# A decoder layer on one core: three more k pairs of the MLP's down product in seven products, and halves added by DMAs

## What is computed

```python
x = _layer_norm(DEEPNORM_ALPHA * x + xa, ln2_g[l], ln2_b[l])
ff = jnp.square(jax.nn.relu(x @ w_ff1[l])) @ w_ff2[l]      # 1024 -> 4096 -> 1024
x = _layer_norm(DEEPNORM_ALPHA * x + ff, ln3_g[l], ln3_b[l])
```

## Time and profile before

| | us |
|---|---|
| median of 3 runs (lowest, highest) | 400.83 (400.57, 403.71) |
| the profiled execution | 401.14 |
| its span, first to last instruction | 399.3 |
| PE, DVE, ACT busy in the span | 390.9, 330.2, 251.3 |

### The profile page before, as it was taken

How to read it: one execution, slowest core, us unless ns; L and a number is a source line. 1 busy time by engine, 2 the same in 40 slices (tenths; PEclk the granted TensorE clock), 3 DMA queues, 4 the chain that set the end, 5 groups by cost and what they waited for, 6 DMA issues and landing times.

```text
span 399.3 us, 5666 instructions
## 1 busy us (share of the span) xinstructions
PE 390.9 (98%) x2118; PEld 334.8 (84%) x2118; DVE 330.2 (83%) x430; ACT 251.3 (63%) x335; POOL 74.1 (19%) x71
## 2 busy tenths in 40 slices
PE   8999999999999999999999999999999999999993
PEld 6888888889888888899988888888888888888872
DVE  5599595999988896878567776999798979999896
ACT  6666569666464628555733776787687767776720
POOL 2059400047860105000005101000000000000000
PEclk9999999999999999999999999999999999999998
DMA  8997737734646390755353266775776575667002
GB/s 286 376 379 264 252 116 249 259 128 139 243 146 213 106 313 5 243 179 191 126 200 126 97 236 213 238 235 214 236 231 190 202 253 175 219 220 251 2 0 105
DMA packets 24449, 78.39 MB, mean 196 GB/s; under 512 B 1670, under 2 KB 3046, under 8 KB 20326
## 3 DMA queue, kind: packets, MB, share of 16 engines
q1 hardware_dynamic: 22592, 75.24, 52.5%
q0 software_dynamic: 1440, 2.62, 4.5%
q10 hardware_dynamic: 390, 0.17, 0.2%
HBM read 76.97 MB, written 1.05 MB: 195 GB/s over the span
## 4 chain that ended last, share of the span: by engine, by line
PE 81%; DMA 8%; DVE 6%; ACT 2%; issue 2%; DVEq 0%; ACTq 0%
PE bank L1560 15%; PE bank L1561 15%; PE bank L1562 15%; PE bank L1634 12%; PE bank L1963 7%; DMA raw<-in_w_ff 7%; PE bank L1638 6%; PE bank L1970 4%; DVE w_lo L1400 2%; PE bank L1786 2%; DVE w_lo L1394 1%; PE bank L1566 1%; DMA raw<-in_lead 1%; PE bank L1740 1%; DVE actB L1462 0%
## 5 line engine op out<-in xcount | busy, mean ns | idle before, releaser
L1011 DVE TENSOR_TENSOR w_lo<-raw,w_hi 128x2048 fp32r<-128x2048 f32 x30 | 70.6, 2360 | 10.9 <-ACT w_hi L609 10.8
L609 ACT CAST w_hi<-raw 128x2048 fp32r<-128x2048 f32 x32 | 60.7, 1913 | 15.9 <-PE bank L1562 14.3
L1963 PE MATMUL bank<-actA,w_hi 128*128 128x512 f32 x224 | 55.6, 391 | 0.0
L1963 PEld LDWEIGHTS bank<-actA,w_hi 128*128 128x128 f32 x224 | 41.9, 188 | 8.9 <-ACT const L918 0.3
L1560 PE MATMUL bank<-w_hi,actB 128*128 128x512 f32 x109 | 43.4, 398 | 0.0
L1561 PE MATMUL bank<-w_lo,actB 128*128 128x512 f32 x109 | 42.7, 391 | 0.0
L1562 PE MATMUL bank<-w_hi,actB 128*128 128x512 f32 x109 | 42.6, 391 | 0.0
L1560 PE MATMUL bank<-w_hi,actA 128*128 128x512 f32 x96 | 38.0, 396 | 0.0
L1562 PE MATMUL bank<-w_hi,actA 128*128 128x512 f32 x96 | 37.5, 391 | 0.0
L1561 PE MATMUL bank<-w_lo,actA 128*128 128x512 f32 x96 | 37.5, 390 | 0.0
L1634 PE MATMUL bank<-actA,w_hi 128*128 128x512 f32 x140 | 34.4, 392 | 0.0
(11 more groups left out here) (241 smaller groups left out, 864.2 us busy)
## 6 DMA issues: line engine op xcount, KB each, us to landing
raw<-in_w_ff SPq DMA_DIRECT2D x32, 1024.0 KB, 6.0
raw<-in_w_in SPq DMA_DIRECT2D x10, 1024.0 KB, 6.9
raw<-in_w_xkv SPq DMA_DIRECT2D x8, 1024.0 KB, 5.0
raw<-in_w_mix_o SPq DMA_DIRECT2D x4, 1024.0 KB, 4.9
raw<-in_w_xq SPq DMA_DIRECT2D x4, 1024.0 KB, 5.0
raw<-in_w_xo SPq DMA_DIRECT2D x4, 1024.0 KB, 5.0
raw<-in_w_ff POOLq DMA_DIRECT2D x10, 256.0 KB, 6.3
raw<-in_lead SPq DMA_DIRECT2D x6, 384.0 KB, 5.4
```

Source lines behind the costliest of these rows:

```text
L609: act.copy(dst, half_view(u)).then_inc(hi_done, 1)
L1011: dve.tensor_tensor(dst, half_view(u), hi_part.bitcast(f32), ALU.subtract).then_inc(lo_done, 1)
L1963: pe.matmul(b[:, :].rearrange("p (h s) -> p h s", h=2), hi[:, k, m * P:(m + 1) * P], actA[:, :, k, :], start=k == 0, stop=False, skip_grou ...
```

## The change

- `KINDS` becomes "CCSSSSSSSSSSSSSL": pairs 5, 9 and 14 are S pairs too, 13 in all, and one L pair is left.
- `add_halves` on DVE stays for pairs 2 and 15 alone. For pairs 3 to 14 POOL issues two DMAs each (`half(p, 0)`, `half(p, 1)`), which add the right 256 columns onto the left ones within SBUF, 128 KB each, when `empty(p, m)` has been done. `square(p)` waits for both (`half_in`). POOL issues them in order with the T3 DMAs.
- The tile `emptied` is doubled; the second one lies where the rows of the last layer norm's scale stood. These rows are loaded late into a `raw` buffer.
- The order within the loops changes. ACT: up_high(q+3), down_high(q+1), empty(q+2, 0), wsum_high(q+1), square(q+1), hidden_high(q+1), empty(q+2, 1). DVE: up_low(q+3), weight_sums(q+1), down_low(q+1), hidden_sums(q+1), wsum_low(q+1), hidden_low(q+1).
- PE has one more step, q = 14, of 21 matmuls without an up block; of the corners 24 matmuls (one pair) are left of 48.

```diff
-KINDS = "CCSSSCSSSCSSSSLL"
+KINDS = "CCSSSSSSSSSSSSSL"
...
-LAST_ORDER = ["P1", "P2", "P6", "P3", "P5", "P7", "P4"]
+LAST_ORDER = ["P1", "P2", "P6", "P5", "P3", "P7", "P4"]
...
-        emptied = const[:, 384:1408].rearrange("p (b n) -> p b n", b=2)
+        emptied_by = [v.rearrange("p (b n) -> p b n", b=2) for v in (const[:, 384:1408], probs[:, 2048:3072])]
+        emptied = emptied_by[0]
...
-            sp.wait_ge(ln_done, 8)
-            load_ln(2)
+            sp.wait_ge(up_lo, PAIRS - 2)
+            sp.dma_start(ln3_rows[:, 0:D], ln3_g.partition_broadcast(P)).then_inc(ln_in[2], 16)
+            sp.dma_start(ln3_rows[:, D:2 * D], ln3_b.partition_broadcast(P)).then_inc(ln_in[2], 16)
...
-            for q in S_PAIRS:
+            def third_sum(q):
+
+                if q >= PAIRS or KINDS[q] != "S":
+                    return
                 r, u = s_rank(q), ff_unit("down", q)
                 pool.wait_ge(raw_in[u % RAW], raw_count(u))
                 pool.dma_start(half_view(u)[:, 1536:2048], w_ff2[q, :, 512:1024], accum_op=ALU.add)\
                     .then_inc(t3_in[r % 2], 16)
+
+            def half(p, m):
+
+                pool.wait_ge(up_free, 2 * (p - 2) + m + 1)
+                v = emptied_by[p % 2][:, m]
+                pool.dma_start(v[:, 0:S], v[:, S:2 * S], accum_op=ALU.add).then_inc(half_in[p % 2], 16)
+
+            third_sum(2)
+            for p in range(3, PAIRS - 1):
+                third_sum(p)
+                half(p, 0)
+                half(p, 1)
+            third_sum(PAIRS - 1)
...
             def square(p):
-                act.wait_ge(halves_added, p - 1)
+                if p in (2, PAIRS - 1):
+                    act.wait_ge(halves_added, 1 if p == 2 else 2)
+                else:
+                    act.wait_ge(half_in[p % 2], 32 * ((p - 3) // 2 + 1))
                 act.wait_ge(a_lo, p - 1)
...
             first_hidden(1)
+            hidden_high(0)
             empty(2, 0)
-            hidden_high(0)
             hidden_high(1)
+            empty(2, 1)
             down_high(1)
-            empty(2, 1)
             for q in range(1, LAST_S):
                 up_high(q + 3)
+                down_high(q + 1)
+                empty(q + 2, 0)
+                wsum_high(q + 1)
                 square(q + 1)
-                empty(q + 2, 0)
-                down_high(q + 1)
                 hidden_high(q + 1)
-                wsum_high(q + 1)
                 empty(q + 2, 1)
-            up_high(LAST_S + 3)
-            square(LAST_S + 1)
-            empty(LAST_S + 2, 0)
-            hidden_high(LAST_S + 1)
-            down_high(LAST_S + 1)
+            square(PAIRS - 1)
+            hidden_high(PAIRS - 1)
             act.wait_ge(wsum_lo, len(S_PAIRS))
             act.wait_ge(product_done, 1)
             act.copy(first_product, bank[P_BANK["P1"]][:, :]).then_inc(p1_copied, 1)
...
             for q in range(1, LAST_S):
+                up_low(q + 3)
                 weight_sums(q + 1)
-                up_low(q + 3)
+                down_low(q + 1)
                 hidden_sums(q + 1)
-                down_low(q + 1)
+                wsum_low(q + 1)
                 hidden_low(q + 1)
-                wsum_low(q + 1)
-                add_halves(q + 2)
-            up_low(LAST_S + 3)
-            hidden_low(LAST_S + 1)
-            down_low(LAST_S + 1)
+            add_halves(PAIRS - 1)
+            hidden_low(PAIRS - 1)
...
-            for n, q in [(0, PAIRS - 2), (1, PAIRS - 2), (0, PAIRS - 1), (1, PAIRS - 1),
-                         (2, PAIRS - 2), (2, PAIRS - 1), (3, PAIRS - 2), (3, PAIRS - 1)]:
-                corner(n, q)
+            for n in range(4):
+                corner(n)
```

More of the change, by code:

```diff
@@ L369, in build @@
         t2_made, t1_t4_made, wsum_hi, wsum_lo = map(sem, ("t2_made", "t1_t4_made", "wsum_hi", "wsum_lo"))
+        half_in = [sem(f"half_in{r}") for r in range(2)]
         halves_added, relu_done, hidden_done, asum_made = map(sem, ("halves_added", "relu_done", "hidden_done", "asum_made"))
@@ L915, in empty @@
                 act.wait_ge(up_full, n + 1)
-                if n >= 2:
-                    act.wait_ge(relu_done, p - 2)
-                act.copy(emptied[:, m], bank[UP_BANK[n] if n < 4 else 7][:, :]).then_inc(up_free, 1)
+                if p >= 4:
+                    act.wait_ge(relu_done, p - 3)
+                act.copy(emptied_by[p % 2][:, m], bank[UP_BANK[n] if n < 4 else 7][:, :]).then_inc(up_free, 1)
             def square(p):
-                act.wait_ge(halves_added, p - 1)
+                if p in (2, PAIRS - 1):
+                    act.wait_ge(halves_added, 1 if p == 2 else 2)
+                else:
+                    act.wait_ge(half_in[p % 2], 32 * ((p - 3) // 2 + 1))
                 act.wait_ge(a_lo, p - 1)
                 v = hidden[p % 2][:, 0:512]
-                act.activation(v.rearrange("p (m s) -> p m s", m=2), emptied[:, :, 0:S], ACT.Relu).then_inc(relu_done, 1)
+                act.activation(v.rearrange("p (m s) -> p m s", m=2), emptied_by[p % 2][:, :, 0:S], ACT.Relu).then_inc(relu_done, 1)
                 act.wait_ge(relu_done, p - 1)
@@ L1432, in add_halves @@
                 dve.wait_ge(up_free, 2 * (p - 2) + 2)
-                dve.tensor_tensor(emptied[:, :, 0:S], emptied[:, :, 0:S], emptied[:, :, S:2 * S], ALU.add)\
+                v = emptied_by[p % 2]
+                dve.tensor_tensor(v[:, :, 0:S], v[:, :, 0:S], v[:, :, S:2 * S], ALU.add)\
                     .then_inc(halves_added, 1)
@@ L1484, in _ @@
             hidden_sums(0)
+            hidden_low(0)
             hidden_sums(1)
-            hidden_low(0)
             hidden_low(1)
@@ L2022, in _ @@
                 order = ORDER if q < LAST_S else LAST_ORDER
-                up_block(q + 2, 0)
+                if q < LAST_S:
+                    up_block(q + 2, 0)
                 if KINDS[q] == "S":
@@ L2027, in _ @@
                     multiply_plain(q, 0)
-                up_block(q + 2, 1)
+                if q < LAST_S:
+                    up_block(q + 2, 1)
                 if KINDS[q] == "S":
@@ L2032, in _, with corner @@
                     multiply_plain(q, 1)
-            def corner(n, q):
+            def corner(n):
                 name, t, c = [("P2", 1, 1), ("P3", 1, 0), ("P7", 0, 0), ("P4", 0, 1)][n]
                 pe.wait_ge(corner_done, n + 1)
[L2038 to L2043, removed]
+                pe.wait_ge(a_lo, PAIRS)
+                pe.wait_ge(up_lo, PAIRS - 1)
+                a = blocks[(PAIRS - 1) % 3]
                 for m in range(2):
                     block_at = (2 * m + t) * P
[L2046 to L2050, removed]
-                    i = three(bank[P_BANK[name]][:, :], [a[:, at0 + block_at:at0 + block_at + P] for at0 in (0, 896)],
-                              mov, False, q == PAIRS - 1 and m == 1, on=True)
-                if q == PAIRS - 1:
-                    i.then_inc(corner_full, 1)
-            for n, q in [(0, PAIRS - 2), (1, PAIRS - 2), (0, PAIRS - 1), (1, PAIRS - 1),
-                         (2, PAIRS - 2), (2, PAIRS - 1), (3, PAIRS - 2), (3, PAIRS - 1)]:
-                corner(n, q)
+                    mov = [v[:, 1, 0, m * 1024 + c * 512:m * 1024 + (c + 1) * 512] for v in (w_hi, w_lo)]
+                    i = three(bank[P_BANK[name]][:, :], [a[:, at0 + block_at:at0 + block_at + P] for at0 in (0, 896)],
+                              mov, False, m == 1, on=True)
+                i.then_inc(corner_full, 1)
+            for n in range(4):
+                corner(n)
 def kernel(**inputs):
```

10 lines of the change are left out of this document (3 added, 7 removed).

## The result

The changed kernel takes 413.86 us (median of 6 runs, 413.42 to 414.65) against 401.06 (6 runs, 400.54 to 403.71): 1.0319 times as long, 95% interval [1.0294, 1.0344]. The profiled execution took 414.18 us. The forecast was 413.4.

The account below looks back on a forecast made before the run. PE was taken to bound the MLP before, a loop of ACT and DVE after: span 399.3 + 8.9 (loop) + 3.7 (tail) = 411.9 us, 413.7 with 1.84 around it, less 0.31 gives 413.4; range 406 to 422.

Parts of the forecast that it names:

- PE's 2.0 us: Pairs 5, 9 and 14 drop from 24 to 21 matmuls on PE, saving 2.0 us that would not show.
- The rival's figure for a PE-bound kernel: Steps stay at PE's 10.35 us: first combination at 383.0, 401 us in all, no change; chance 0.13.
- The loop of 11.35 us: Eight waits or engine-order links between ACT and DVE, up_high to next up_high, make each iteration 11.35 us; chance 0.70.
- PE's idle time of 1.0 us a step: PE waits for ACT's copy empty(q+2, 1) before each step's first up block, standing still 1.0 us.
- the margin: PE's slack before it wants bank 7 back: 2.05 us less 0.58 for the copy, used up in two iterations.
- The start: Iteration 1's weight sums start between 245.9 and 248.1, taken as 247.5, so iteration 2 opens at 254.7 us.
- The tail: Last up_high to first combination 15.9 us, then 16.4 to the end; 3.7 us longer than before.
- The halves land in time: Each half's DMA within SBUF may take 7.2 us before square needs it; nothing added for the DMAs.
- The range's worry (8.1 us): Halves as slow as the slowest 1 MB load delay square, some 424 us; late halves' chance 0.12, port lock included.
- The weight buffers have room: Load, T3, weight sums, down_low and issue take 18.6 us against two iterations of 22.7; T3 has 4 us spare.
- The chain of before: In the kernel before, the MLP steps' chain of waits goes through DVE and the weight buffers, not PE.
- The port lock on POOL's issues: Two-port DVE instructions block POOL's descriptor writes, delaying halves by 2.28 us more: 445 us; chance 2 in 100.

Follow-up runs that it names:

- square_first: Changed kernel with down loads first, DVE's weight_sums first, up_low mostly ahead of hidden_low, and ACT's square ahead of wsum_high; 402.17 us, ratio 1.0017.
- (4): Changed kernel with empty(q+2, 1) moved ahead of hidden_high(q+1) on ACT; 408.39 us.
- (5): Changed kernel with wsum_high(q+1) moved behind hidden_high(q+1) on ACT; 429.09 us.
- two_c: Changed kernel with pairs 5 and 9 as C pairs again, 6 matmuls more; 410.98 us.
- (7): Same run as two_c: changed kernel with pairs 5 and 9 as C pairs again; 410.98 us.
- (1): Changed kernel with weight_sums(q+1) moved ahead of up_low(q+3) on DVE; 415.13 us, ratio 1.0343.
- (11): Changed kernel with down loads first, DVE's weight_sums first, up_low ahead of hidden_low; last up_low on POOL, last wsum_low ahead of hidden_low and add_halves; 408.52 us.
- sums_first: Same run as (1): changed kernel with weight_sums(q+1) ahead of up_low(q+3) on DVE; 415.13 us.
- (12): Same run as square_first: down loads first, DVE's weight_sums first, ACT's square ahead of wsum_high, against the changed kernel; 402.17 us.
- (6): Changed kernel with the loops of ACT and DVE in the order of the kernel before, halves still by DMA; 430.61 us.

## Why the prediction was right

- *PE's 2.0 us are worth nothing.* Right in both forms. In the changed kernel PE idles more than it saves; in `square_first`, where it doesn't, DVE's tail takes it. The rival's figure for a PE-bound kernel, a first combination at 383.0 and 401 us, was met at 382.94 and a span of 399.3, in a kernel that keeps the change's parts and loses its loop. That both agree to 0.1 us is partly chance: this kernel opens its second iteration at 253.68, not 255.33, has another order at its end, and one iteration waits for a half.
- *The loop of 11.35 us.* Measured 11.345. By the starts above its eight terms are 1.94, 2.21, 2.05, 1.39, 1.31, 1.12, 0.85 and 0.47, each within 0.03 of the forecast's. Two experiments moved single terms: 0.48 out gave 10.86 (4), and the order of `wsum_high` gave a longer walk, of 12.46 (5). That each link is a wait or an engine's order, which the prediction set against the rival, held.
- *PE's idle time of 1.0 us a step.* It is 0.99, of which the trace shows 0.7 as idle. It begins at 278.19, when the margin is used up.
- *The start.* Iteration 2 opened at 255.33, forecast 254.7. The weight sums began at 248.14, the upper of the two bounds (248.1), where I had taken 247.5 in between. This is the one term that was mis-sized, by 0.6 us, and nearly the whole distance between the forecast and the result: `up_low(4)` did go first, at 245.94. T3 was not what held it until then. DVE had waited 1.33 us for ACT's `down_high(1)` and was busy with `down_low(1)` and `add_halves(2)` up to that moment.
- *The tail.* From the last `up_high` 15.87 us to the first combination (forecast 15.9) and 16.4 to the end (16.4). The waits of ACT on DVE and back that were to stand in a row there do.
- *The halves land in time.* Right as a sum, for a reason told too simply. `half(p, 1)`, the one with 7.2 us to go, landed in 3.2 to 4.4 us (the last one in 2.6). `half(p, 0)`, issued just behind T3, took 7.1 to 8.4, mostly above T3's longest of before (7.5); but it has 14.7 us to go (361.05 + 0.59 to the next iteration's `square`, 11.35 behind 365.03), so that it didn't matter. The range's worry (8.1 us) was real for the wrong one of the two. T3 itself took 4.4 to 7.9.
- *The weight buffers have room.* Right for this order as to DVE: from 250 us on T3 lands 3.8 us or more ahead of the weight sums, near the 4 us forecast. But I gave the same 4 us to `down_high`, which needs T3 too and starts 1.8 us into the iteration. It had only 1.5 to 1.7 us to spare in six of twelve iterations, and in `two_c` nothing (7). With `up_low` between the sums and `down_low`, and loads of 8 to 9.4 us, a round takes 24.2 and binds in one iteration of three (1). How much loads and T3 lengthen when they fall together was missing in the room that I gave.
- *The chain of before.* The prediction lets it go through DVE and the buffers, not through PE. That holds from 321.84 us on; its rows from 270 to 321 are PE's matmuls. The sum uses nothing of this.
- *The port lock on POOL's issues.* 852 to 864 ns beside a DVE that was nearly full, and up to 1218 only just behind the issue of a T3: not there, as argued. A POOL instruction that reads SBUF is another matter (11).

Open: why the loads lengthen to over 9 us in `sums_first`, of which the halves explain a part only; and what makes PE's clock fall, since equal rests of 1.8 us did it in some steps and not in others. The parts of the change were taken out of the changed kernel, never put one by one into the kernel before; so what thirteen S pairs cost with the order of before and the halves on DVE is not known. A shorter tail, the only way to a gain by these rows, was tried once (11) and not reached.

## What to carry to other kernels

Where two engines hand work back and forth in order, walk each ring from start to start, through waits and queue order alike, before you count busy time: the longest ring is the iteration's floor, however idle the engines are, and an edit is worth what it changes in that ring, as long as no other is longer. After cutting it, look for the next one at once (here 11.35, then 11.5 on average through the buffers, or 10.63, then PE's 10.35), for it may be longer than the one cut. And freeing the busiest engine pays only if the end of the kernel is its own: here thirteen S pairs at PE's pace (12) gained nothing, since the last 16.4 us are DVE's.

## What the runs showed of the hardware

- At 0.7 us of idle time a step PE's granted clock stayed 1.00. Rests of 1.8 to 1.9 us (5) were followed by a lower one in four of seven steps (0.66 in one window; eight matmuls of 512 columns took 3.54 us, at full clock 2.11), a single rest of 3.35 us (6) was not. In a loop that PE didn't bound the lower clock cost nothing (5).
- A 128x2048 float32 subtraction takes POOL 4.91 us and DVE 2.28, and a `tensor_tensor` of DVE that started 0.4 us behind POOL's was held up for nearly as long (1.08 became 5.42). One case (11).
- An accumulating DMA of 128 KB within SBUF landed in 2.6 to 4.4 us when the one ahead of it on POOL's queue had been issued some 4 to 7 us earlier, and in 7.1 to 8.4 when it was issued 0.5 to 1.3 us behind one of 256 KB.
